# Gates as three-pass tiles between state products of half the size, rows turned in four partition groups, and modulations at other places in a two-block kernel

## What is computed

```
def first_block(x, c, ...):
    c_act = silu(c)
    for l in range(2):
        shift, scale, gate = split(c_act @ w_mod[l] + b_mod[l], 3)
        h = x * (1 + scale) + shift
        y = diff_attention(h, a_w_in, ...)  if l == 0 else forgetting_attention(h, b_w_in, ...)
        x = layer_norm(DN_ALPHA * x + gate * y, ln_g[l], ln_b[l])

def diff_attention(h, w_in, w_out, ...):
    q, k, v, g = split(h @ w_in, 4)
    ...
    return (rms_norm(o) * silu(g)) @ w_out

def second_block(x, c, ctx, c_ctx, ...):
    sh1, sc1, gt1, sh2, sc2, gt2 = adaln(c, w_mod, b_mod)
    csh1, csc1, ... = adaln(c_ctx, w_mod, b_mod)
    h_lat = modulate(rmsnorm(x, norm_mix_pre), sh1, sc1)
    h_ctx = modulate(rmsnorm(ctx, norm_mix_pre), csh1, csc1)
    y = s5_mixer(h_ctx, h_lat, ...)     # states of 128 groups, both directions, context first, then GLU
    x = x + gt1 * rmsnorm(y)
    x = x + gt2 * rmsnorm(sq_relu_mlp(modulate(rmsnorm(x), sh2, sc2), w1, w2))
```

## Time and profile before

| | |
|---|---|
| median of 3 runs | 3047.95 us (3038.79 to 3049.62) |
| the profiled execution | 3041.96 us, its span 3040.2 us |
| PE busy | 2642.3 us, 87% |
| DVE busy | 1536.8 us, 51% |
| ACT busy | 1121.0 us, 37% |
| mean granted clock of PE | 0.893 |

### The profile page before, as it was taken

The page is one execution under the profiler, slowest core; times in us unless marked ns, Lnnn a source line. Parts: engine busy times, 40 slices in busy tenths (PEclk is TensorE's granted clock), DMA queues, the critical chain, the costliest instruction groups (busy, mean ns, idle before and its releaser), DMA issues.

```text
span 3040.2 us, 42300 instructions
## 1 busy us (share of the span) xinstructions
PE 2642.3 (87%) x17961; PEld 2126.6 (70%) x17961; DVE 1536.8 (51%) x2274; ACT 1121.0 (37%) x1765; POOL 164.4 (5%) x239
## 2 busy tenths in 40 slices
PE   5599998877857969989999985787969999999996
PEld 1388876445445758769875665666859899898995
DVE  4457877254445665433323443716455545555554
ACT  0253333322134323333332333725444444344443
POOL 1102335000000000000000001000000000000000
PEclk8699999778778979989997895798989999999998
DMA  9869999655377858867886574894544555555552
GB/s 356 264 210 356 345 375 378 210 199 200 142 280 256 303 182 309 309 239 252 317 318 221 194 249 130 187 266 126 184 133 139 184 190 185 193 185 190 190 184 80
DMA packets 333531, 699.85 MB, mean 230 GB/s; under 512 B 14016, under 2 KB 34976, under 8 KB 326944
## 3 DMA queue, kind: packets, MB, share of 16 engines
q1 hardware_dynamic: 313248, 625.17, 61.2%
q0 software_dynamic: 15216, 65.69, 5.9%
q10 hardware_dynamic: 4880, 6.29, 0.9%
HBM read 638.38 MB, written 54.53 MB: 228 GB/s over the span
## 4 chain that ended last, share of the span: by engine, by line
PE 73%; DVE 11%; DMA 9%; ACT 4%; issue 2%; SPq 1%; ACTq 0%; DVEq 0%; POOL 0%
PE bank L1929 71%; DVE arena L1238 4%; DMA ring<-in_w_mod 3%; PE bank L1932 3%; DMA ring<-in_a_w_in 2%; DVE ring_lo L1238 2%; DVE arena L1246 2%; ACT L812 1%; DMA arena<-proj 1%; DVE LT L1246 1%; DMA ring<-in_a_w_out 1%; ACT arena L815 0%; DMA arena<-in_ctx 0%; DMA arena<-arena 0%; SPq L685 0%
## 5 line engine op out<-in xcount | busy, mean ns | idle before, releaser
L1238 DVE TENSOR_TENSOR ring_lo<-ring,w_hi 128x1024 fp32r<-128x1024 f32 x320 | 390.1, 1225 | 423.4 <-ACT w_hi L862 422.7
L862 ACT CAST w_hi<-ring 128x1024 fp32r<-128x1024 f32 x320 | 334.7, 1049 | 460.3 <-PE bank L1929 460.2
L1238 DVE TENSOR_TENSOR ring_lo<-ring,att_w_hi 128x1024 fp32r<-128x1024 f32 x192 | 230.7, 1222 | 317.2 <-ACT att_w_hi L862 316.9
L862 ACT CAST att_w_hi<-ring 128x1024 fp32r<-128x1024 f32 x192 | 198.1, 1050 | 399.3 <-PE bank L1929 125.7
L1929 PE MATMUL bank<-in_hi,w_hi 128*128 128x256 f32 x1024 | 291.1, 284 | 2.2 <-issue 2.2
L1929 PE MATMUL bank<-in_lo,w_hi 128*128 128x256 f32 x1024 | 290.9, 284 | 0.0
L1929 PE MATMUL bank<-in_hi,ring_lo 128*128 128x256 f32 x1024 | 290.8, 284 | 0.0
L1929 PE MATMUL bank<-ring,cpad 128*32 128x512 f32 x1792 | 243.1, 680 | 44.1 <-DMA ring<-in_w_mod 41.4
L1932 PE MATMUL bank<-ident,arena 128*128 128x128 f32 (+2 forms) x739 | 121.0, 335 | 161.6 <-DVE arena L1238 49.2
L1932 PEld LDWEIGHTS bank<-ident,arena 128*128 128x128 f32 (+2 forms) x739 | 101.3, 194 | 179.9 <-issue 59.2
L815 ACT COPY arena<-bank 128x512 f32<-128x512 f32 (+2 forms) x200 | 113.5, 619 | 278.0 <-PE bank L1929 211.7
(11 more groups left out here) (220 smaller groups left out, 5135.4 us busy)
## 6 DMA issues: line engine op xcount, KB each, us to landing
ring<-in_w_mod SPq DMA_DIRECT2D x192, 1024.0 KB, 11.2
ring<-in_a_w_in SPq DMA_DIRECT2D x64, 1024.0 KB, 8.5
ring<-in_w_mlp_in SPq DMA_DIRECT2D x64, 1024.0 KB, 5.2
ring<-in_w_mlp_out SPq DMA_DIRECT2D x64, 1024.0 KB, 5.1
ring<-in_kv_w_mod SPq DMA_DIRECT2D x32, 1024.0 KB, 9.6
ring<-in_b_w_in SPq DMA_DIRECT2D x32, 1024.0 KB, 6.7
ring<-in_kv_w SPq DMA_DIRECT2D x32, 1024.0 KB, 6.5
ring<-in_s_w_glu SPq DMA_DIRECT2D x32, 1024.0 KB, 5.3
```

The source lines that it names most:

```text
L862: a.copy(whi(h), raw_half(h)).then_inc(*o.up("whi"))
L1238: return v.tensor_tensor(dst, x, y, op).then_inc(*(to or o.up("dve")))
```

## The change

Four things are changed.

1. **Gates.** Panels 12 to 15 become 64 three-pass tiles like those of panels 0 to 11, with high parts in a buffer of their own (`PG`, four places). Panel 12 lies in the context rows: eight tiles ahead of the sums, one ahead of each `u_turn`. Panels 13 to 15 lie in the state products, two tiles in each of the pieces 1 to 8, 11 to 18 and 21 to 28.
2. **State products.** 32 pieces `b` of 4 values of d, with operations of 512 elements, and two buffers (`bls`) in place of one. The tables of banks follow. Writes of `m_state` are 32 of half the size.
3. **Rows.** Context and latent rows are laid in 128 partitions, four groups of 32, by DMAs on POOL's queue (8 for the context; 16 for the latent rows, 8 behind each half of the layer norm). The row scale is computed for eight rows of each partition (`square`, `u_norm`: 8 squares on ACT, one matmul of sums on PE), and applied as the data are turned within the partition (`turn`: 8 operations on DVE, 8 on ACT). `u_turn` is 16 plain matmuls with the identity, 32 partitions each, instead of 16 transposes. The modulation is applied behind it (`u_piece`, two operations of DVE a piece), with factors that PE prepares once (`fu`, 32 small matmuls). The broadcasts `ctx_a`, `ctx_b`, `lat_a`, `lat_b` and the DMAs on ACT's queue go.
4. **Modulations and the rest.** Panels 8 and 10 of 0 to 11 have no modulation; the state products have 8 (0, 9, 10, 19, 20, 29, 30, 31) instead of 5; attention A none (4); steps 3, 14 to 19, 21 and 23 none; layer norm 0 has 3, layer norm 1 has 5 (two ahead of the row sums, three behind `u_turn`), MLP steps 55 to 58 one each. In the first stage six of eight banks of the input are turned ahead of modulation 7, and the state data b and c load behind modulation 7's chunks instead of behind modulation 6's. `split_in` makes the high and low part one round later, beside the next turn. The projections for attention A are loaded earlier in part, POOL makes the masks at piece 30, and DVE's and ACT's first splits of step 4 stand beside `split_in("q")`.

```diff
+MOD_AT_PRE = {**{pn: 8 + pn for pn in range(8)}, 9: 16, 11: 17}
+MOD_AT_BL = {0: 18, 9: 19, 10: 20, 19: 21, 20: 22, 29: 23, 30: 24, 31: 25}
+MOD_AT_STEP = {0: 26, 1: 27, 2: 28, **{n: 28 + n for n in range(4, 14)}, 55: 52, 56: 53, 57: 54, 58: 55}
+MOD_AT_LN, LN1_BEFORE = ((29, 30, 31), (47, 48, 49, 50, 51)), 2
...
+U_TILES = 8
+G_TILES = {1 + 10 * p + s: (16 * (N_PRE + 1 + p) + 2 * s, 16 * (N_PRE + 1 + p) + 2 * s + 2) for p in range(3) for s in range(8)}
...
 # SP
-            sp.wait_ge(*filled("vc", 14))
-            sp.wait_ge(S["ms0"], 16 * 8)
+            sp.wait_ge(*filled("proj", 15, 1))
             sp.dma_start(reg(12288, 4096), proj_d[1]).then_inc(S["p1"], 16)
...
 # ACT: rows
+                act(MSB[:, 0:512].rearrange("p (e n) -> p e n", e=2), HC[:, :, q, :], ACT.Square,
+                    *o.up("sq" if q == 7 else "act"), accum_out=ssu[:, q:q + 1])
...
+                        act(dst[:, e], src[:, e], ACT.Copy, *o.up("turn_a" if e else "act"), scale=rsu[:, q:q + 1])
...
 # ACT: state products
-            for ch in range(17):
-                if ch in GATE_OUT_BL:
-                    project(GATE_OUT_BL[ch])
-                if ch:
-                    v_out(("vc", ch - 1), Vc[:, :, :, 8 * ch - 8:8 * ch], 8 * ch - 8)
...
+            for b in range(33):
...
+                for r in range(2 if b < 32 else 0):
+                    a.wait_ge(*filled("bl", b, r))
+                    copy(vmats[b % 2][:, :, r, :], bank("bl", b, r)[:, :].rearrange("p (d m) -> p d m", d=4), *empty("bl", b, r))
+                if b:
+                    v_out(("vc", b - 1), Vc[:, :, :, 4 * b - 4:4 * b], 4 * b - 4)
+                for i in range(*G_TILES.get(b + 1, (0, 0))):
+                    tile(i)
+                if b in MOD_AT_BL:
+                    mod(MOD_AT_BL[b])
...
 # DVE: state products
             def bl(b):
+                if b > 1:
+                    v.wait_ge(*filled("bl", b - 2, 1))
+                for _ in cmul(Bb[:, 0], Bb[:, 1], L2v, 4, 8, 4 * b, *bls[b % 2], bt, False, "blm"):
+                    pass
+
+            bl(0)
+            tiles(G_TILES[1][1])
+            bl(1)
+            for b in range(1, 32):
...
+                if b + 1 in G_TILES:
+                    tiles(G_TILES[b + 1][1])
+                if b < 31:
+                    bl(b + 1)
...
 # PE: rows
-                    t = tr(bank("u", run, pc)[:, 32 * j:32 * j + 32],
-                           hc_turned(run, pc)[0:32, j, :, :].rearrange("p q h -> p (q h)"), k=32)
+                    t = mm(bank("u", run, pc)[:, 32 * j:32 * j + 32], HT[run][at, e, j, :, :].rearrange("p q h -> p (q h)"),
+                           ident[at, at], True, True)
...
 # PE: state products
+            for b in range(33):
+                if b < 32:
+                    p.wait_ge(S["blm"], b + 1)
+                    for r in range(2):
+                        room("bl", b, r)
+                        for j in range(4):
+                            t = tr(bank("bl", b, r)[:, 128 * j:128 * j + 128], bls[b % 2][r][:, 128 * j:128 * j + 128])
+                        t.then_inc(*fill("bl", b, r))
+                for i in range(*G_TILES.get(b, (0, 0))):
+                    pre_tile(i)
+                if b:
+                    p.wait_ge(*emptied("bl", b - 1, 1))
+                    if b == 1:
+                        p.wait_ge(S["u_made"], 8)
+                    v_chunk(("vc", b - 1), vmats[(b - 1) % 2], U, 4 * (b - 1))
...
 # PE: layer norm 1
-            bcast("lat_a", acol2)
-            bcast("lat_b", M("m2", 0))
-            sums(MOD_END["m2c"])
-
+            for j in MOD_AT_LN[1][:LN1_BEFORE]:
+                mod(j)
+            u_sums(1)
             for pc in range(8):
                 u_turn(1, pc)
-            p.wait_ge(*emptied("u", 1, 7))
+            for j in MOD_AT_LN[1][LN1_BEFORE:]:
+                mod(j)
```

More of the change, by code:

```diff
@@ L117, in step, with tile @@
             bank.use(("step", n, b), GD)
[L119 to L123, removed]
+    def tile(i):
+        pn, k = divmod(i, 16)
+        if k == 0:
             for b in range(2):
-                bank.use(("proj", pn, b), GD)
+                bank.use(("proj", pn, b), GD if pn < N_PRE else GL)
+        if k % 4 == 0:
+            ring.use(("proj", pn, k // 4), slots)
     for i in range(3):
@@ L1045, in v_out @@
+            turn(0)
+            for i in range(NG + 8, 16):
+                tile(16 * N_PRE + i)
+            project(2 * N_PRE)
+            a.wait_ge(*filled("u", 0, 7))
+            project(2 * N_PRE + 1)
             def v_out(key, dst, d0):
-                bv = bank(*key)[:, :].rearrange("p (d r c) -> p d r c", r=2, c=32)
+                n = dst.shape[-1]
+                bv = bank(*key)[:, 0:64 * n].rearrange("p (d r c) -> p d r c", r=2, c=32)
                 dv = dst if d0 < 64 else dst[:, ::-1]
@@ new lines, in u_norm, with turn @@
+            def u_norm(run):
+                v.wait_ge(*filled("ss", run))
+                copy(varu, bank("ss", run)[:, 0:8], *empty("ss", run))
+                own()
+                ts(varu, varu, 1.0 / D, 1e-6, MUL, ADD, *o.up("var"))
+                newton(rsu, varu, tmpu, (0, 4)[run], *o.up("rstd"))
+            def turn(run):
+                v.wait_ge(S["rstd"], run + 1)
+                for q in range(0, 8, 2):
+                    src, dst = row_of(run, q)
+                    for e in range(2):
+                        ts(dst[:, e], src[:, e], rsu[:, q:q + 1], None, MUL, None, *o.up("turn_v" if e else "dve"))
@@ L1831, in vector_program @@
             layer_norm(1)
[L1833 to L1835 removed]
+            u_norm(1)
+            turn(1)
+            for pc in range(8):
+                u_piece(1, pc)
+            mod_bias("m2b")
             for f in range(2):
@@ L1956, in mod @@
             def mod(j):
-                if j and j - 1 != MOD_END["m0s"]:
+                if j and j - 1 not in [MOD_END[g_] for g_ in SUMMED]:
                     sums(j - 1)
@@ L1967, in mod, with turn_in @@
                     t.then_inc(*(fill("mod", j) if q == 3 else (S["taken"], 1)))
-            def turn_in(which, src):
-                for k2 in range(8):
+            def turn_in(which, src, part=range(8)):
+                for k2 in part:
                     key = ("xt", which, k2)
```

655 lines of the change are left out of this document (315 added, 340 removed).

## The result

The changed kernel takes 3268.3 us (median of 4, 3265.3 to 3282.4) against 3047.3: ratio 1.074, 95% interval 1.070 to 1.078. The direction was forecast, the size was not: +221 us where +113 was predicted, and 3268 lies above the forecast range of 3080 to 3205. The profiled span is 3265.8 us, 225.6 more than before.

The account below looks back on a forecast made before the run. PE, busy 87% of the span, was taken as the bound, so only shortening stretches where PE waits would win. Terms summed to +115 on the profiled 3042, 3157, with the median at 3160 us; range 3080 to 3205.

Parts of the forecast that it names:

- State products, +163: State products and gates: 21 rounds in series of 15.4 us plus 88 make 411 us against 248 before.
- The three orders: State products: on PE, ACT and DVE, work ahead in program order puts everything after v_chunk(b-1) in series; PE idles 6.7 us.
- the 0.6 to 0.7 that I had named as a sign: State products: expected mean clock in the changed profile, with the stage lasting some 410 us.
- rival A: State products: same series but the clock stays high, rounds of 12.1 us, +94 instead of +163, 3091 us; chance 0.13.
- Rival B: State products: no series, DVE sets the pace, stage 192 us, -56 instead of +163, 2945 us; chance 0.09.
- Rows in four groups, -15 and +38: Rows in four partition groups: context stage takes 76 us against 91 (-15); in the latent rows V begins near 1909, not 1870 (+38).
- the way back to transposes: u_turn: its 16 pieces should have stayed transposes; plain matmuls priced at up to 30 us in all, about half exposed.
- Rival C: Gains outside the state products loop missed (low clock in context, late state data), +25 and +8, rounds of 16.1 (+15): 3205 us.
- The start: First stage: state data now wait for modulation 7, six of eight banks turned before it: -14 (-6 to -18).
- the split stages: Three split stages go one step further in parallel, 3 us each: -9.
- The eight modulations taken out of steps 4 to 23: Modulations leave steps 14 to 19 (six, -28) and steps 21 and 23 (two, -9), where PE had no gap.
- the first term: State products and gates, +163; without it the change was said to be worth -48.

## Why the prediction was right in kind and wrong in size

**State products, +163: right (+152).** The three orders showed a series, and it is there. Of a round, PE's idle time is 6.62 us (forecast 6.7) and its work 7.0 (forecast 8.5): the clock rises within every round's tiles (the pitch of 512 columns goes from 0.43 to 0.23 us), so a round is 13.6 and not 15.4. 21 x 1.8 is 38 us less than forecast; the rest of the stage is 400 - 21 x 13.6 = 114 instead of 88. That the term came within 11 us is in part luck, for these two errors have opposite signs. The stage's mean clock is 0.76, above the 0.6 to 0.7 that I had named as a sign. The round lies between the forecast and rival A (12.1), which was nearer than I allowed. Rival B is out for this kernel, and it names the fault exactly: with the casts free of v_chunk the stage is 237 us. That is 45 more than rival B's 192. A round with two tiles takes 6.0 us on average there (4.9 to 6.7), not 5.3, which is 18 of it over 24 pieces; the rest lies at the pieces with modulations, which wait for chunks, and behind which PE stands 7.8 us for DVE twice.

**Rows in four groups, -15 and +38: wrong, +54 and +70.** The step that failed is the sentence "A plain f32 matmul is two records (the 16 of a half panel stand as x32), so a piece takes 3.76". It took the number of records from one row and the price of a record from a transpose. The price of a plain record is 0.19 to 0.22 us, so a piece takes 6 to 7 at the low clock. The run with transposes took 38 us out of the context stage and 37 out of the latent one. The prediction had itself named the way back to transposes, and priced it at up to 30 us over both runs; it is worth 74.

The record to take was one whose weights are as wide. The 64 records of the factors have 128*128 weights and 16 columns and take 3.56/16 = 0.22 us each; 32*128 weights and 32 columns take 0.214 in the kernel before. The Trainium skill (TensorE: Matmul & The Clock Gate, section LDWEIGHTS) says just this: loading weights takes time by the number of their columns, not of their rows, so that 32 rows by 128 columns cost as much as 128 by 128. These two rows agree. The transposes can't say: 0.118 a record with 32 rows against 0.246 with 128, both at the low clock, but these differ also in the columns that are multiplied (32 and 128). It was from the 0.118 that I priced.

By the trace, the context's error of 69 us is made up of:
- u_turn, 50 us for eight pieces against 8 x 2.2: +33 (the run with transposes, 1.9 us a piece, gave back 38)
- the factors, 64 records, which were not priced at all, 13.6: with them the first piece starts 47.8 us after the modulation and not 33: +15
- the order of DVE, low part behind `u_piece`, which was not read: seven waits of 2.11, +15
- the tiles between them, mostly at the low clock, 2.86 us each and not 1.37: +12
- the end, 8.4 us where 14 stood in the sum: -6

The third is the same fault as in the state products, which I had looked for there and not here.

In the latent run, 19 of the 32 us missed are u_turn (49 against 30). Another 8 are its later start: the rows landed 22 us after the norm instead of 10, of which the norm and the squares gave back 4. The modulations behind u_turn took 4 more. The forecast of the landing went by the old rows, where PE began after the first transfers of 128 KB; now it begins only when all 2.1 MB are there. The two runs on it say that of 28 us 20 are the rows' own and 8 the ring's chunks beside them. On such transfers the Trainium skill (DMA: Bandwidth & Descriptors, section Why small descriptors are slow) holds that those within SBUF do not suffer from small descriptors. Nothing here speaks against it: in the kernel before the rows went in packets of 1 KB and cost half as much of the DMA engines' time as now in packets of 4 KB. Smaller packets were not run, and what slows the new transfers stays open.

Rival C looked for losses outside of the loop, and they were there, but it gave them 33 us by the clock and the state data; 101 came, and of C's causes only the low clock of the tiles (12) shows.

**Smaller terms.** The start gave more (-24 for -14), the panels too. From attention A to step 23, 27 us less than forecast came: layer norm 0 is 10 us longer and not 2, with one wait of 7.6 us for a chunk of its three modulations, and the split stages gave nothing that shows. The eight modulations taken out of steps 4 to 23 gave less than their 37 us. A part of this, and of the MLP, is a slower pace of the matmuls of 512 columns at the full clock. Their starts lie 0.231 to 0.233 us apart in the changed kernel and in the runs made from it, and 0.227 to 0.228 in the kernel before and in the run made from that one. For the 1536 in the MLP that is an estimated 7 us, less 3 that the matmuls of 256 columns gain (0.119 against 0.120). Why is not known. In the MLP 6.5 of the 12 us missed are PE's wait for ACT's copy of the last modulation's rows:

```profile
3121.55 1.87 PE L1966 MATMUL bank<-sel,mod_rows 128*128 128x1 f32 x8 [6.51 <-ACT mod_rows L829]
```

The forecast that it would be 48 us faster without the first term is wrong too: 226 - 152 is +74. Only with u_turn as transposes (-74) is the rest about even.

## What to carry to other kernels

Where two engines take turns, write down for each engine what stands ahead of the work that the other waits for. Here two lines on a third engine, ACT, were worth 160 us, and a second buffer nothing. Price an instruction from a row of the same form and the same width of weights: a transpose is no measure for a plain matmul of the same shape, nor the other way round. When the series is found in one stage, look for it in every other stage that the change writes anew.

## What the runs showed of the hardware

- A plain f32 matmul of 32 rows by 128 columns of weights takes two records of 0.19 to 0.22 us at the low clock, a transpose of the same shape one of 0.118 (16 in 1.88 us): 3.6 times as much, or four times by the distance of two starts (0.213 and 0.107 us a record). Near the high clock 32 such records took 3.9 and 4.1 us (changed kernel), and 16 transposes 1.18 us (the run on the order in the context rows).
- PE was busy without a gap for 49 us on 256 such records, and for 55 us on V's, and the granted clock stayed at 0.50; in the state products it rose within the 12 matmuls of 512 columns of each round.
- A DVE operation on two elements a partition took 3.52 and 4.80 us beside POOL's memsets, each ending with a memset, and 0.17 without them; operations with two inputs in between took 0.35 us for two, as without the memset.
- 2.1 MB of rows moved within SBUF in 16 DMAs on POOL's queue, as 512 packets of 4 KB, held the DMA engines at full share for 17 us, at 110 GB/s (115 at best). The same bytes in 16 DMAs on ACT's queue, as 2048 packets of 1 KB, took the equivalent of 9 us.
- With casts on a third engine in the way, DVE and PE took turns at 13.6 us a round with two buffers as with one; with the casts moved ahead, the round was 6.0 us, again with either.
